# Two experts of one token in each gathered row block: expert sums with a 128-row contraction in a two-layer transformer kernel

## The chip, the cores and the metric

The kernel runs on one core of a Trainium2 chip, as one launch. The metric is the device time of that launch in microseconds, lower is better. All data are float32 (indices uint32).

## The reference

Two transformer layers run on 512 tokens of width 1024. Each layer has a mixer (layer 1: a state-space model and sliding-window attention; layer 2: a sparse attention and a short convolution) and then a retrieval of experts, which is what the change touches. For each token, 8 heads select 16 of 16,384 experts; with u and v the experts' rows of 1024 numbers:

```python
q = (xt @ w_query).reshape(t, PEER_HEADS, 2, PEER_KEY_DIM // 2)
s = einsum('thkd,hknd->thkn', q, sub_keys)
vals, idx = top_k(s, 16)                        # for each half of the key
best, pos = top_k(all 256 sums of the two halves' values, 16)
expert = i1 * 128 + i2 ; gate = softmax(best)   # 8 heads x 16 = 128 experts a token
a = einsum('cd,ced->ce', xb, u_tab[expert])     # one dot product per expert
w = gate * gelu(a)
out = einsum('ce,ced->cd', w, v_tab[expert])    # a weighted sum of the v rows
```

## The kernel before

The program is written by hand for each engine, and engines wait on semaphores. 512 tokens are 4 blocks of 128, two layers make 8 blocks n = 0..7, and each block has 128 **slots**, k = 0..127: 1024 slots in all, numbered s = 128 n + k.

One slot is one expert of each of the block's 128 tokens, with token p on partition p:

1. GpSimd (POOL) issues one indirect DMA that fetches 128 rows of 8 KB, u and v of an expert side by side, into a ring (L2263). It may do so when `idx` of the head is there, when `dot(s - 5)` is done (5 u places) and when `vmm(s - 10)` is done (10 v places).
2. VectorE (DVE) computes the dot product of the u row with the token's normalized input `xn` in one custom instruction (L409, function `dot`).
3. ScalarE (ACT) takes the gelu for a pair of slots and makes from it `diag`, a 128 x 64 tile: row p holds the weight in column p mod 64 and zeros elsewhere (`weigh`; all ACT activations stand under line L1198). `ident2` is the identity's two column halves added, and `gid` is `ident2` scaled by the gate.
4. TensorE (PE) multiplies `diag` by the v rows and adds into two PSUM banks (`vmm`, L1623). Tokens 0-63 and 64-127 are contracted apart, and the 1024 columns are taken in two halves, so a slot is four matmuls of 64 rows by 64 columns by 512, each on its own quarter of the array (`tile_position`). Every float32 matmul stands in the trace as two instructions and two weight loads: 8 and 8 a slot.

Beside the slots the same engines compute the mixers, the projections and the selection of the next blocks' experts. The order is fixed: `place` gives each part of that work a slot number, and `pace` and `slots` run the slots up to it first. TensorE runs four slots (`VL`) behind the dot products. SyncE streams weights of 512 KB into 6 places.

The parts that the change touches:

- `route(n)` (layer 1) and `route2(a)` (layer 2, two blocks at once) make X, the normalized input of block n, transpose it, project it and score it. X stands in `xn[:, n % 3, :]`.
- `top_part(n, h, q)` selects a head's 16 experts; its last instruction writes `idx` (L890). `gates(n, h)` writes `gate` (L466 in the profile, after a reciprocal in L856). On DVE `chained` and `wait_own` wait for the instruction before.
- the buffers `bmod`, `bmod2`, `cact` and `mrow` (a modulation vector, computed in block 0) lie in `xn`.

Of the kernel before, what the change touches and what calls it, by code (L numbers as in the profile page):

```python
# [104 lines left out]
def build(nc, A, out, act_counts):  # L105
    ctx = ExitStack()
    with ctx:
# [38 lines left out]
        xn = sb("xn", [128, 3, D])  # L146
# [63 lines left out]
        bmod2 = xn[:, 1, :].rearrange("p (a b) -> p a b", b=128)  # L210
        bmod, o = carve(xn[:, 2, :], 0, 4, 128)
        cact, o = carve(xn[:, 2, :], o, 8, 32)
        mrow = [carve(xn[:, 2, :], o + 128 * k, 128)[0] for k in range(2)]
# [185 lines left out]
        def vector_program(v):  # L399
            V = Lane("v", v, sems, book)  # L400

            def dot(s):
                n, k = divmod(s, 128)
                b = n % 2
                V.stage("dot")
                V.wait_ge("fetch", s)
                if k == 0 and n >= 2:
                    V.wait_ge("diag", 128 * (n - 1) - 1)
                V(v.tensor_tensor_reduce(u_row(s), u_row(s), xn[:, n % 3, :], 1.0, 0.0, ALU.mult, ALU.add,  # L409
                                         aw[:, b, k:k + 1]), ("dot", s))  # L410

# [27 lines left out]
            def slots(x):  # L439
                back = V.here  # L440
                while V.slot < x and V.slot < END:
                    c = V.slot
                    V.slot += 1
                    n, k = divmod(c, 128)
                    if c < NSLOT:
                        dot(c)
                    if c - 1 in turn_at:
                        finish(turn_at[c - 1])
                    if c in last_at:
                        finish2(last_at[c])  # L450
                    for m, h, q in tops.get(c, ()):
# [367 lines left out]
            def route(n):  # L819
                X = xn[:, n % 3, :]  # L820
                pace(n, "route", 0.0)
                V.stage("route")
                if n == 2:
                    V.wait_ge("modo", 10)
                    V.wait_ge("modo", 11)
# [10 lines left out]
                V(v.tensor_copy(xT[:, 4:8, :], P3(1)), ("XT", n, 1))  # L836
                pace(n, "route", 0.6)
# [12 lines left out]
            def gates(n, h):  # L850
                R = RB[n // 4]
                V.stage("top")
                V.wait_ge("g_exp", n, h)
                if h == 0 and n >= 2:
                    V.wait_ge("gid", 128 * (n - 1) - 1)
                V(v.reciprocal(R["zs"][:, h:h + 1], R["zs"][:, h:h + 1]))  # L856
                chained(lambda: ts(gate[:, n % 2, 16 * h:16 * h + 16], R["best"][:, h, :], R["zs"][:, h:h + 1], None,
                                   ALU.mult, None), ("gate", n, h))

            def top_part(n, h, q):  # L860
# [21 lines left out]
                if q == 3:  # L882
# [7 lines left out]
                    chained(lambda: v.scalar_tensor_tensor(idx[:, b, 16 * h:16 * h + 16], ee[:, 0, :], 128.0, ee[:, 1, :],  # L890
                                                           ALU.mult, ALU.add), ("idx", n, h))
# [233 lines left out]
            def route2(a):  # L1125
# [6 lines left out]
                for j in range(2):  # L1132
                    n = a + j
                    X = xn[:, n % 3, :]
# [8 lines left out]
                for j in range(2):  # L1143
                    n = a + j
                    pace(a, "route", 0.25 + 0.08 * j)
                    V.stage("route")
                    V.wait_ge("X_t", n, 1)
                    V(v.tensor_copy(XT[:, 4:8, 128 * j:128 * j + 128], P3((5, 3)[j])), ("XT", n, 1))
                for b in range(2):
# [43 lines left out]
        def scalar_program(a):  # L1193
# [32 lines left out]

            def evacuate(n):
# [26 lines left out]
            def slots(x):  # L1254
                back = S.here
                while S.slot < x and S.slot < END:
# [9 lines left out]
                    if c in last_at:  # L1266
                        finish2(last_at[c])
                    for m, h in exps.get(c, ()):
# [119 lines left out]
            def route(n):  # L1388
# [9 lines left out]
                S(act(xT[:, 0:4, :], P3(0), ACT.Copy), ("XT", n, 0))  # L1398
                if n == 0:
# [12 lines left out]
                pace(n, "route", 1.0)  # L1412

# [15 lines left out]
            def norm2(a):  # L1429
# [7 lines left out]
                S.stage("norm")  # L1437
                for j in range(2):
# [112 lines left out]
            def route2(a):  # L1551
# [7 lines left out]
                for j in range(2):  # L1559
# [4 lines left out]
                    S(act(XT[:, 0:4, 128 * j:128 * j + 128], P3((4, 2)[j]), ACT.Copy), ("XT", n, 0))  # L1564
                for b in range(2):
# [41 lines left out]
        def tensor_program(t):  # L1607
            T = Lane("t", t, sems, book)

            def vmm(s):  # L1610
# [294 lines left out]
            def route(n):  # L1905
                X = xn[:, n % 3, :]
# [252 lines left out]
            def route2(a):  # L2159
# [6 lines left out]
                for j in range(2):  # L2166
                    n = a + j
                    X = xn[:, n % 3, :]
# [314 lines left out]
```

## Time and profile before

| what | value |
|---|---|
| time, median of 3 runs | 3346.07 us (3346.05 to 3347.88) |
| the profiled execution | 3346.05 us, span of its instructions 3344.3 us |
| TensorE (PE) matmuls | 2489.2 us busy, 74% of the span |
| VectorE (DVE) | 2324.1 us, 69% |
| ScalarE (ACT) | 1328.9 us, 40% |
| GpSimd (POOL) | 1139.9 us, 34% |
| DMA | 1295.01 MB, mean 387 GB/s |
| mean granted TensorE clock | 0.836 |

A busy time is the time in which at least one instruction of the engine runs. Matmuls overlap, so their mean durations don't add up to it. The DMA share is the mean busy share of the core's 16 DMA engines; in dense stretches it reads slightly over 1. The granted clock is a share of 2.4 GHz: 0.5 is the level of 1.2 GHz and 1.0 that of 2.4 GHz.

### The profile page before, as it was taken

The numbers are of one execution on the slowest core, as the hardware profiler recorded it, in microseconds if no ns is written. First come the engines' busy times: TensorE is split into PE (matmuls) and PEld (weight loads), VectorE is DVE, ScalarE is ACT, GpSimd is POOL, SyncE is SP. The second block draws the span as 40 slices with busy tenths as digits, with TensorE's granted clock in tenths as the row PEclk, the third lists the DMA queues.
The fourth block names the chain that finished last, engine by engine and source line by source line (L and its number), as shares of the span: only waits on it lengthen the run. The fifth ranks groups of instructions, "written<-read, shape, count | busy, mean of one in ns | idle before, by whom it ended". The sixth has DMA issues, their size and how long they took to land.

```text
span 3344.3 us, 40597 instructions
## 1 busy us (share of the span) xinstructions
PE 2489.2 (74%) x14052; PEld 1065.7 (32%) x14052; DVE 2324.1 (69%) x5515; ACT 1328.9 (40%) x3602; POOL 1139.9 (34%) x1038
## 2 busy tenths in 40 slices
PE   8787778787797877969788759778887656555555
PEld 3443233223332233326343416423333211111111
DVE  6518785697947878385885585887866777777644
ACT  1213542444324444243473353357843343333322
POOL 0001343324323244242333343343433444444432
PEclk9698879898798987989788979877888877777776
DMA  7689999999999999999999999999999999999997
GB/s 228 204 305 393 417 394 406 405 409 414 383 394 418 414 404 382 404 399 385 371 381 393 382 408 365 413 411 416 369 409 363 406 420 419 418 410 414 419 420 323
DMA packets 214057, 1295.01 MB, mean 387 GB/s; under 512 B 26934, under 2 KB 30294, under 8 KB 82776
## 3 DMA queue, kind: packets, MB, share of 16 engines
q0 software_dynamic: 148320, 1076.50, 79.8%
q1 hardware_dynamic: 64860, 213.81, 16.9%
q8 instruction: 110, 1.80, 0.2%
q10 hardware_dynamic: 672, 2.12, 0.2%
q14 instruction: 95, 0.78, 0.1%
HBM read 1289.62 MB, written 2.71 MB: 386 GB/s over the span
## 4 chain that ended last, share of the span: by engine, by line
PE 34%; DMA 27%; DVE 21%; issue 9%; ACT 4%; POOL 3%; another core or an unknown queue 0%; POOLq 0%; ACTq 0%; DVEq 0%; SPq 0%
DMA ring<-in_k_uv,idx 11%; DMA ring<-in_k_vu,idx 11%; PE ps L1623 11%; PE ps L1703 10%; DVE ring L409 9%; DMA wsl<-in_k_wu 5%; PE ps L1959 5%; POOL ring L2263 3%; PE ps L1969 2%; DVE big L462 2%; ACT L1198 1%; PE ps L1680 1%; PE ps L1850 1%; DVE pers L462 1%; ACT diag L1198 1%
## 5 line engine op out<-in xcount | busy, mean ns | idle before, releaser
L1623 PE MATMUL ps<-ring,diag 64*64 64x512 f32 x8192 | 1264.4, 745 | 485.4 <-ACT diag L1198 460.0
L409 DVE CUSTOM_DVE_ANT_0 ring<-ring,xn 128x1024 f32<-128x1024 f32 x1024 | 1238.6, 1221 | 486.1 <-DMA ring<-in_k_vu,idx 260.2
L2263 POOL DMA_INDIRECT ring<-in_k_vu,idx x514 | 570.7, 1110 | 1144.0 <-DVE aw L409 635.5
L2263 POOL DMA_INDIRECT ring<-in_k_uv,idx x510 | 563.0, 1104 | 960.0 <-DVE aw L409 656.4
L1623 PEld LDWEIGHTS ps<-ring,diag 64*64 64x64 f32 x8192 | 315.6, 159 | 1266.6 <-ACT diag L1198 737.0
L1198 ACT ACTIVATE aw<-aw 128x2 f32<-128x2 f32 x512 | 103.7, 203 | 1086.2 <-DVE aw L409 1082.5
L1703 PE MATMUL ps<-wsl,xT 128*128 128x512 f32 x896 | 437.6, 633 | 31.5 <-DMA wsl<-in_k_wu 28.7
L1198 ACT ACT_TABLE_LOAD x338 | 433.7, 1283 | 11.9 <-DVE fin L436 5.2
L1198 ACT ACTIVATE diag<-gid,aw 128x64 f32<-128x64 f32 x1024 | 311.1, 342 | 302.1 <-PE ps L1623 285.1
L1198 ACT ACTIVATE gid<-ident,gate 128x64 f32<-128x64 f32 x1024 | 292.5, 333 | 0.0
L1703 PEld LDWEIGHTS ps<-wsl,xT 128*128 128x128 f32 x896 | 168.9, 199 | 296.6 <-issue 234.0
L1959 PE MATMUL ps<-pers,wsl 128*128 128x256 f32 x896 | 208.7, 393 | 25.1 <-DVE pers L467 17.8
L1959 PEld LDWEIGHTS ps<-pers,wsl 128*128 128x128 f32 x896 | 173.6, 196 | 72.0 <-issue 48.0
L1850 PE MATMUL ps<-pers,rowB 128*128 128x64 f32 x224 | 51.4, 422 | 72.3 <-DVE rowB L708 49.1
L409 DVE DVE_READ_ACCUMULATOR2_ANT aw<- 128x1 f32 x1024 | 84.6, 83 | 0.0
L1198 ACT ACTIVATE big<-ps 128x512 f32<-128x512 f32 (+4 forms) x58 | 30.2, 537 | 123.8 <-PE ps L1703 107.7
L1850 PEld LDWEIGHTS ps<-pers,rowB 128*128 128x128 f32 x224 | 48.8, 329 | 83.9 <-issue 83.9
L462 DVE TENSOR_TENSOR big<-ps,big 128x512 f32<-128x512 f32 x16 | 11.1, 692 | 78.4 <-PE ps L1703 78.4
L462 DVE TENSOR_TENSOR big<-big 128x512 f32<-128x512 f32 x68 | 47.1, 692 | 19.3 <-ACT big L1198 17.1
L1703 PE MATMUL ps<-wsl,fin 128*128 128x512 f32 x128 | 59.0, 604 | 0.9 <-DMA wsl<-in_k_wu 0.9
L2119 PE MATMUL ps<-pers 128*128 128x64 f32 x320 | 49.7, 307 | 12.4 <-DVE pers L1069 12.4
L2093 PE MATMUL ps<-pers,big 64*128 64x128 f32 (+3 forms) x128 | 54.8, 540 | 5.0 <-DVE big L462 5.0
(249 smaller groups left out, 2170.2 us busy)
## 6 DMA issues: line engine op xcount, KB each, us to landing
wsl<-in_k_wu SPq DMA_DIRECT2D x342, 512.0 KB
wsl<-in_k_wmod SPq DMA_DIRECT2D x48, 512.0 KB
ring<-in_k_vu,idx POOLq DMA_INDIRECT x514
ring<-in_k_uv,idx POOLq DMA_INDIRECT x510
wsl<-in_k_wu SPq DMA_DIRECT2D x8, 280.0 KB
hres<-in_x SPq DMA_DIRECT2D x4, 512.0 KB, 7.5
pers<-L1d POOLq DMA_DIRECT2D x8, 256.0 KB, 13.6
out<-fin ACTq DMA_DIRECT2D x4, 512.0 KB, 2.6
```

The costliest lines, as they stand in the source:

```text
L409: V(v.tensor_tensor_reduce(u_row(s), u_row(s), xn[:, n % 3, :], 1.0, 0.0, ALU.mult, ALU.add, aw[:, b, k:k + 1]), ("dot", s))
L462: return v.tensor_tensor(out, a_, b_, op)
L1198: return a.activation(out, in_, f, **kw)
L1623: r = t.matmul(PA[half][64 * q:64 * q + 64, :], diag[64 * half:64 * half + 64, s % (2 * PAIR), :], v_row(s)[64 * half:64 * half + 64, 512 ...
L1680: r = t.transpose(PS[bank][:, at + j * 128:at + (j + 1) * 128], s_, ident[:, :])
L1703: r = t.matmul(PS[bank][:, 0:nn], lhsT(kk_), wsl[:, at % NWS, j, 0:nn], start=(kk_ == 0 and not offset), stop=(kk_ == nk - 1))
L1850: x = t.matmul(PS[4 + h // 8][:, 64 * (h % 8):64 * (h % 8) + 64], PT1[:, r, 128 * k:128 * k + 128], v1[:, (n + 1 + k) % 2, 64 * g:64 * g + ...
L1959: r = t.matmul(PS[banks[c // 2]][:, 256 * (c % 2):256 * (c % 2) + 256], wsl[:, at % NWS, i, 128 * c:128 * c + 128], XT[:, kk_, :], start=( ...
L1969: r = t.matmul(PS[banks[j]][:, 0:nn], left(kk_)[:, 128 * j:128 * j + 128], wsl[:, at % NWS, i, 0:nn], start=(kk_ == 0), stop=(kk_ == nk - 1))
L2093: r = t.matmul(PS[k % 2][:, (h - h0) * Wk:(h - h0 + 1) * Wk], q2T[64 * g:64 * g + 64, h % 4, 128 * j:128 * j + 128], ksT[64 * g:64 * g + 6 ...
L2119: r = t.matmul(PS[4 + br][:, 64 * h:64 * h + 64], PT2[:, k % 2, at:at + 128], vsn[:, m, 128 * br + 64 * g:128 * br + 64 * g + 64], start=( ...
L2263: Q(p.indirect_dma_start(out=both_rows(s), out_offset=None, in_=tab, in_offset=bass.IndirectOffsetOnAxis(ap=idx[:, n % 2, k:k + 1], axis=0 ...
```

## The change

A slot now holds two experts of each of 64 tokens, no longer one expert of each of 128. In a head's 16 slots, the first 8 serve tokens 0-63: partitions 0-63 hold their experts c = 0..7, and partitions 64-127 the same tokens' experts 8..15. The other 8 slots serve tokens 64-127. `diag` already has two rows per column (p and p + 64), so one matmul over all 128 rows now adds both experts of a token. `vmm` issues two matmuls of 128 rows by 64 columns by 512 in place of four of 64 by 64 by 512.

For that, `idx` and `gate` have one quadrant moved between partition halves (three instructions in place of one for each, with waits). Each block's X needs two more versions, tokens 0-63 doubled and tokens 64-127 doubled: `doubled(n, half)` in `xd`, four rows of 1024 in place of three. For n = 0 to 4 and 6 they are made in the route part by `doubled_high` (ACT, one copy) and `doubled_low` (DVE, two copies). For n = 5 and 7 X waits in `xr`, and `doubled_late` makes them at the third slot of block n - 1 (ACT two copies, DVE two copies). Number and size of the gathers, dot products and diagonals stay.

```diff
-        xn = sb("xn", [128, 3, D])
+        xd = sb("xd", [128, 4, D])
...
+        def doubled(n, half):
+            return xd[:, 2 * (n % 2) + half, :]
...
-                if k == 0 and n >= 2:
-                    V.wait_ge("diag", 128 * (n - 1) - 1)
-                V(v.tensor_tensor_reduce(u_row(s), u_row(s), xn[:, n % 3, :], 1.0, 0.0, ALU.mult, ALU.add,
+                if k == 0:
+                    V.wait_ge("xb", n)
+                    if n >= 2:
+                        V.wait_ge("diag", 128 * (n - 1) - 1)
+                V(v.tensor_tensor_reduce(u_row(s), u_row(s), doubled(n, k // 8 % 2), 1.0, 0.0, ALU.mult, ALU.add,
                                          aw[:, b, k:k + 1]), ("dot", s))
+            def doubled_low(n):
+                X = doubled(n, 0)
+                V.wait_ge("X_t", n, 1)
+                V(v.tensor_copy(doubled(n, 1)[0:64, :], X[64:128, :]), ("xl", n))
+                V.wait_ge("xb0", n)
+                V.wait_own()
+                V(v.tensor_copy(X[64:128, :], X[0:64, :]))
+            def doubled_late(n):
+                V.stage("late")
+                V(v.tensor_copy(doubled(n, 0)[64:128, :], xr[0:64, :]))
+                V(v.tensor_copy(doubled(n, 1)[0:64, :], xr[64:128, :]), ("xl", n))
...
-                chained(lambda: ts(gate[:, n % 2, 16 * h:16 * h + 16], R["best"][:, h, :], R["zs"][:, h:h + 1], None,
-                                   ALU.mult, None), ("gate", n, h))
+                V.wait_own()
+                def out(p, to, c, src):
+                    g_ = gate[to:to + p, n % 2, 16 * h + c:16 * h + c + (16 if p == 128 else 8)]
+                    e_ = R["best"][src:src + p, h, 8 - c:16 - c] if p == 64 else R["best"][:, h, :]
+                    return ts(g_, e_, R["zs"][src:src + p, h:h + 1], None, ALU.mult, None)
+                V(out(128, 0, 0, 0))
+                V.wait_own()
+                V(out(64, 64, 0, 0))
+                V(out(64, 0, 8, 64), ("gate", n, h))
...   (idx in top_part: the same three instructions, in place of one)
+            def doubled_high(n):
+                S.wait_ge("X", n)
+                S(act(doubled(n, 1)[64:128, :], doubled(n, 0)[64:128, :], ACT.Copy), ("xb", n), ("xb0", n))
...   (ScalarE's doubled_late: waits for X and for dot 128 (n - 1) - 1, two such copies from xr)
-                for c in range(2):
-                    for half in range(2):
-                        q = (half + c) % 2
-                        r = t.matmul(PA[half][64 * q:64 * q + 64, :], diag[64 * half:64 * half + 64, s % (2 * PAIR), :],
-                                     v_row(s)[64 * half:64 * half + 64, 512 * q:512 * q + 512], start=(k == 0),
-                                     stop=(k == 127), tile_position=(64 * half, 64 * q))
+                half = k // 8 % 2
+                for q in range(2):
+                    r = t.matmul(PA[half][64 * q:64 * q + 64, :], diag[:, s % (2 * PAIR), :],
+                                 v_row(s)[:, 512 * q:512 * q + 512], start=(k in (0, 8)),
+                                 stop=(k in (119, 127)), tile_position=(0, 64 * q))
```

## Rows read from the trace of the kernel before

**Rows 1.** The page: busy engines, and DMA queues (packets, MB, share of 16 engines).

```profile
PE 2489.2 (74%) x14052; PEld 1065.7 (32%) x14052; DVE 2324.1 (69%) x5515; ACT 1328.9 (40%) x3602; POOL 1139.9 (34%) x1038
...
q0 software_dynamic: 148320, 1076.50, 79.8%
q1 hardware_dynamic: 64860, 213.81, 16.9%
```

**Rows 2.** Stretches: length, busy time (instructions) per engine, granted clock, DMA share, GB/s.

```profile
280.00:3322.00 3042.00, 2269.19 (x12671) 949.27 (x12669) 2187.49 (x5173) 1278.38 (x3494) 1128.96 (x1019) 0.84 0.99 401
3160.00:3320.00 160.00, 93.06 (x512) 21.04 (x508) 78.38 (x129) 40.55 (x160) 59.76 (x63) 0.73 1.01 420
```

**Rows 3.** Groups by form: busy us, mean ns of one, idle time before and its releasers.

```profile
L1623 PE MATMUL ps<-ring,diag 64*64 64x512 f32 x8192 | 1264.4, 745 | 485.4 <-ACT diag L1198 460.0 <-ACT xT L1198 16.8 <-ACT big L1198 6.8
L409 DVE CUSTOM_DVE_ANT_0 ring<-ring,xn 128x1024 f32<-128x1024 f32 x1024 | 1238.6, 1221 | 486.1 <-DMA ring<-in_k_vu,idx 260.2 <-DMA ring<-in_k_uv,idx 210.5 <-issue 14.3
```

**Rows 4.** Timeline of TensorE in five places: start us, length us, how many instructions.

```profile
3304.24 3.69 PE L1623 MATMUL ps<-ring,diag 64*64 64x512 f32 x16 [1.30 <-ACT diag L1198]
3309.21 1.95 PE L1623 MATMUL ps<-ring,diag 64*64 64x512 f32 x16 [1.28 <-ACT diag L1198]
...
549.50 1.09 PE L1623 MATMUL ps<-ring,diag 64*64 64x512 f32 x8
550.52 3.70 PE L1703 MATMUL ps<-wsl,xT 128*128 128x512 f32 x8
...
167.80 1.52 PE L1870 MATMUL ps<-wsl,xn 128*32 128x128 f32 x48
```

**Rows 5.** Groups by form again: small VectorE writes, copies on VectorE and ScalarE.

```profile
L890 DVE SCALAR_TENSOR_TENSOR idx<-rowB 128x16 uint32<-128x16 f32 x32 | 5.6, 175 | 1.1
...
L466 DVE TENSOR_SCALAR gate<-rowB 128x16 f32<-128x16 f32 x32 | 7.5, 234 | 1.3 <-DVE rowB L856 0.2
...
L623 DVE COPY big<-big 128x512 f32<-128x512 f32 x4 | 1.7, 427 | 0.1
...
L1198 ACT ACTIVATE xr<-hres 128x1024 f32<-128x1024 f32 x14 | 14.7, 1048 | 56.6 <-DVE hres L462 42.7 <-DVE xn L462 11.5 <-DMA hres<-in_x 2.4
```

**Rows 6.** Timeline of VectorE around the first indices and gates.

```profile
256.06 0.69 DVE L889 TENSOR_REDUCE rowB<-rowB 128x32 f32<-128x512 f32 x1
256.78 0.17 DVE L890 SCALAR_TENSOR_TENSOR idx<-rowB 128x16 uint32<-128x16 f32 x1
256.88 0.48 DVE L462 TENSOR_TENSOR xn<-ps,xn 128x128 f32<-128x128 f32 x2
...
266.63 0.23 DVE L466 TENSOR_SCALAR gate<-rowB 128x16 f32<-128x16 f32 x1
266.78 0.29 DVE L462 TENSOR_TENSOR xn<-ps,xn 128x128 f32<-128x128 f32 x1
274.70 0.29 DVE L462 TENSOR_TENSOR xn<-ps,xn 128x128 f32<-128x128 f32 x1 [7.64 <-PE ps L1870]
```

**Rows 7.** Stretches, columns as in rows 2: two selections, three where the DMA share falls.

```profile
283.00:359.00 76.00, 73.03 (x245) 25.66 (x244) 72.17 (x246) 34.38 (x76) 17.25 (x18) 0.95 0.98 397
686.00:755.00 69.00, 57.52 (x203) 19.00 (x202) 63.30 (x211) 31.13 (x70) 14.88 (x16) 0.90 1.02 408
...
1480.00:1500.00 20.00, 12.48 (x57) 8.78 (x58) 18.61 (x52) 7.44 (x21) 6.18 (x5) 0.74 0.92 370
...
2000.00:2020.00 20.00, 14.67 (x64) 10.58 (x65) 15.65 (x46) 4.51 (x14) 6.36 (x6) 0.74 0.77 286
2540.00:2560.00 20.00, 15.02 (x92) 5.40 (x88) 17.20 (x41) 8.09 (x21) 7.86 (x6) 0.73 0.66 234
```

**Rows 8.** Timeline of all engines in the route part of blocks 6 and 7.

```profile
2535.33 3.78 PE L1711 MATMUL ps<-big,ones 1*128 1x512 f32 x4 [12.22 <-DVE big L1130]
...
2541.81 1.22 DVE L409 CUSTOM_DVE_ANT_0 ring<-ring,xn 128x1024 f32<-128x1024 f32 x1
...
2543.31 0.94 POOL L2263 DMA_INDIRECT ring<-in_k_vu,idx  x1 [10.45 <-DVE aw L409]
```

More of the change, by code:

```diff
@@ L209, in build @@
         av = xr
[L210 to L213, printed above, removed]
+        bmod2 = xd[:, 2, :].rearrange("p (a b) -> p a b", b=128)
+        bmod, o = carve(xd[:, 3, :], 0, 4, 128)
+        cact, o = carve(xd[:, 3, :], o, 8, 32)
+        mrow = [carve(xd[:, 3, :], o + 128 * k, 128)[0] for k in range(2)]
         hn = cols2[:, 0:20]
@@ L450, in slots @@
                         finish2(last_at[c])
+                    if k == 2 and n in L2_PARTS:
+                        doubled_late(n + 1)
                     for m, h, q in tops.get(c, ()):
@@ L819, in route @@
             def route(n):
-                X = xn[:, n % 3, :]
+                X = doubled(n, 0)
                 pace(n, "route", 0.0)
                 V.stage("route")
-                if n == 2:
-                    V.wait_ge("modo", 10)
-                    V.wait_ge("modo", 11)
                 rstd(n, "r", 1, D)
@@ L836, in route @@
                 V(v.tensor_copy(xT[:, 4:8, :], P3(1)), ("XT", n, 1))
+                if n == 1:
+                    V.wait_ge("modo", 10)
+                    V.wait_ge("modo", 11)
+                doubled_low(n)
                 pace(n, "route", 0.6)
@@ L889, in top_part, with out @@
                     chained(lambda: v.tensor_reduce(ee, oh, AXX, ALU.add))
-                    chained(lambda: v.scalar_tensor_tensor(idx[:, b, 16 * h:16 * h + 16], ee[:, 0, :], 128.0, ee[:, 1, :],
-                                                           ALU.mult, ALU.add), ("idx", n, h))
+                    V.wait_own()
+                    def out(p, to, c, src):
+                        i_ = idx[to:to + p, b, 16 * h + c:16 * h + c + (16 if p == 128 else 8)]
+                        e_ = ee[src:src + p, :, 8 - c:16 - c] if p == 64 else ee
+                        return v.scalar_tensor_tensor(i_, e_[:, 0, :], 128.0, e_[:, 1, :], ALU.mult, ALU.add)
+                    V(out(128, 0, 0, 0))
+                    V.wait_own()
+                    V(out(64, 64, 0, 0))
+                    V(out(64, 0, 8, 64), ("idx", n, h))
             def top(n, h, at):
@@ L1148, in route2 @@
                     V(v.tensor_copy(XT[:, 4:8, 128 * j:128 * j + 128], P3((5, 3)[j])), ("XT", n, 1))
+                pace(a, "route", 0.45)
+                V.stage("route")
+                doubled_low(a)
                 for b in range(2):
@@ L1225, in weigh, with doubled_late @@
                         gated(PAIR * g + PAIR + j)
+            def doubled_late(n):
+                S.stage("late")
+                S.wait_ge("X", n)
+                S.wait_ge("dot", 128 * (n - 1) - 1)
+                S(act(doubled(n, 0)[0:64, :], xr[0:64, :], ACT.Copy))
+                S(act(doubled(n, 1)[64:128, :], xr[64:128, :], ACT.Copy), ("xb", n))
             def evacuate(n):
@@ L1267, in slots @@
                         finish2(last_at[c])
+                    if k == 2 and n in L2_PARTS:
+                        doubled_late(n + 1)
                     for m, h in exps.get(c, ()):
@@ L1398, in route @@
                 S(act(xT[:, 0:4, :], P3(0), ACT.Copy), ("XT", n, 0))
+                if n == 1:
+                    S.wait_ge("modo", 10)
+                    S.wait_ge("modo", 11)
+                doubled_high(n)
                 if n == 0:
@@ L1437, in norm2 @@
                 S.stage("norm")
+                if a == 6:
+                    S.wait_ge("xl", a - 1)
                 for j in range(2):
@@ L1905, in route @@
             def route(n):
-                X = xn[:, n % 3, :]
+                X = doubled(n, 0)
                 pace(n, "route", 0.0)
```

7 lines of the change are left out of this document (5 added, 2 removed).

## The prediction

> **What bounds the kernel now.** I read the page first, for who is busy, then the stretches, for what is full when, and then the timeline, because a busy share doesn't say who waits for whom. The page shows no engine full: TensorE 74%, VectorE 69%. The two DMA queues together show 79.8 + 16.9 = 96.7% of all 16 engines' span [rows 1]. The stretches say the same by time. From 280 us, when the gathers are running, to the last gather at 3322 us, the DMA share is 0.99; from 3160 to 3320 us, where slots alone run, it is 1.01 at 420 GB/s, which is what "full" reads like here [rows 2]. Its 512 matmul instructions, at 8 a slot, are 64 slots in 160 us: 2.5 us a slot, while VectorE is busy 78 us of the 160 and TensorE 93 us [rows 2]. Of the 486 us in which VectorE stands idle before dot products, 471 end with the landing of a gather [rows 3]. So a slot costs the time to fetch 1 MB, and the kernel is bound by its 1295 MB. What can be won between 280 and 3322 us without moving fewer bytes is what is missing from full: (1.01 - 0.99) x 3042 = 61 us by rounded shares. From the stretches where the share falls I read off (1.01 - 0.92) x 20 = 1.8, (1.01 - 0.77) x 20 = 4.8 and (1.01 - 0.66) x 20 = 7.0 us [rows 7]; the holes are short and scattered over the routes and projections. An edit to the slots can thus win little, and it loses only if it delays gathers so far that the queue runs dry.
>
> **TensorE: matmuls halved, time kept.** The edit removes half of the L1623 matmuls (8 to 4 instructions a slot, 8192 to 4096) [rows 3]. What matters is how the old ones run. At the full clock, one slot's 8 instructions take 1.09 us, two slots' 16 take 1.95 us, so a further slot adds 0.86 us; 8 instructions over the whole array (128 by 128) take 3.70 us one after the other, a pitch of about 0.43 us [rows 4]. 0.86 is two such pitches: the four quarter-array matmuls already run side by side, in two rounds (a float32 matmul is two instructions). The new slot has two half-array matmuls, each again two instructions of 512 columns, hence again two rounds if the halves run side by side. Do they? No 128 by 64 pair is in the trace. The nearest row is L1870, 128 rows by 32 columns on four column positions: 48 instructions of 128 columns take 1.52 us [rows 4]. A pitch for 128 columns is 0.43/4 = 0.11 us; 48 in a row would need 5.2 us; 12 rounds of four need 1.3 us and the tail of the last one, which is the 1.52. So column positions with all 128 rows do run side by side, four of them. Bounds: below, two rounds less what half the issue could save, at the least one round, 0.43 us, a slot; above, no overlap, 4 x 0.43 = 1.72 us. I take 0.86, no change, as L1870 is very near. At the 1.2 GHz level two slots take 3.69 us [rows 4], and I expect the same there.
>
> The Trainium skill, "TensorEngine Tiling (Array Packing)", section Performance Considerations, "Instruction Overhead", says that each matmul carries some 60 cycles of overhead. By it, four instructions fewer a slot would save 240 cycles, an estimate of 0.10 us at 2.4 GHz, 102 us of TensorE time over 1024 slots. The rows speak against adding that up: 0.86 us for two rounds leaves no room for it. If the rule held, the faster rival below would be the outcome.
>
> **VectorE: index and gate.** For each of 64 heads (8 blocks x 8), `idx` gets two more writes and one wait, `gate` the same. One `idx` write is 0.175 us, one `gate` write 0.234 us [rows 5]. They overlap what follows if it doesn't depend on them: the instruction after `idx` starts 0.10 us after it, the one after `gate` 0.15 us; a dependent one starts 0.03 us after the end (256.06 + 0.69 to 256.78) [rows 6]. So `idx` goes from 0.10 to 0.175 + 0.035 + 0.10 + 0.10 = 0.41 us, +0.31; `gate` from 0.15 to 0.234 + 0.035 + 0.15 + 0.15 = 0.57, +0.42. Without any overlap they would be +0.385 and +0.50. I take 0.75 us a head (0.73 to 0.89), 48 us in all.
>
> **Copies.** Six routes with two VectorE copies and one ScalarE copy, two late ones with two and two: 16 VectorE and 10 ScalarE copies of 64 x 1024. Nearest: 128 x 512 within SBUF at 0.427 us, so 0.8 us for twice the columns; ScalarE 128 x 1024 at 1.05 us [rows 5]. That makes 13 us on VectorE and 10.5 us on ScalarE. `doubled_low` also waits for ScalarE's copy (`xb0`); ScalarE issues it right after its own transposed copy, so 0 to 1 us. Behind the waiting VectorE stand the next dot products, and behind these the gathers five slots on.
>
> **What of these 61 us of VectorE work shows.** A gather has to be issued before the queue is empty, so a delay counts only where VectorE has no idle time to absorb it and the queue has no gather waiting.
>
> - The start. The first gather waits for the first head's `idx`: +0.3 us. Gates and second head add 1.2 us more, but VectorE then idles 7.64 us for TensorE [rows 6]. 0.3 us (0 to 1.5).
> - The selection of six heads during the input projection of blocks 1 to 3. Here VectorE is the tightest: 72.2 of 76 us busy, 63.3 of 69 [rows 7], and the rest is gaps between chained instructions. Six heads add 4.5 us each time. Yet the DMA share is 0.98 to 1.02 meanwhile [rows 7], since weights fill in, and TensorE (73.0 of 76) is nearly full too. Were nothing hidden it would cost 3 x 4.5 = 13.5 us, and all hidden 0. The full DMA decides: I take 1 us each, 3 us.
> - The six routes. 1.6 us of copies and up to 1 us of wait. In the last one the queue does run dry: VectorE waits for TensorE's L1711, the dot product follows at 2541.81, the gather is issued after 10.45 us [rows 8], and the share is 0.66 [rows 7]. The copies come after this hole, when gathers are being caught up. 0 to 2.6 us each, at most 16; I take 2 us for all six.
> - The other selections run beside slots that leave VectorE idle about half the time [rows 2]. The late copies come 126 slots before their use, and so does each wait for `xb` at a block's first dot product, whose X is made in the route before. The wait for `modo`, moved from the route of block 2 to that of block 1 (about 590 us), is for small writes of block 0, whose last matmuls (L1870) ended before 274.7 us [rows 6]. All of these 0.
>
> Were the cover gone everywhere, all 61 us would show. ScalarE at 40% [rows 1] has room for its 10.5 us.
>
> Sum: the profiled execution took 3346.05 us, 3344.3 of span and 1.75 around it; the median of the runs is 3346.07, the same. 3346.05 + 0 + 0.3 + 3 + 2 = 3351.35. I say **3351 us**, 0.15% above. A change within 0.2% (6.7 us: 3339.4 to 3352.8) is about what a measurement of this kernel cannot tell from none.
>
> **The rivals.**
>
> - *TensorE unchanged, VectorE's additions mostly hidden* (forecast): 3343 to 3353, as the holes of the queue may shift by a few us either way.
> - *VectorE's additions uncovered* (slower). For it: 95% busy in the selection and queues that do run dry in routes. Against: full DMA in the same stretches. It gives up to 1.5 + 13.5 + 16 = 31 us, 3377; half of it 3362. It decides from 7 us of uncovered work, a ninth of the 61.
> - *TensorE gets shorter per slot* (faster): if the half-array matmuls needed fewer than two rounds, up to 0.43 us a slot. For it: gathers also wait for vmm(s - 10), and in the hole at 2000 us TensorE is busy 14.7 of 20 us with VectorE at 15.7 [rows 7], so that either may be what is late. It would fill the holes of 1480 and 2000 us, 1.8 + 4.8 us, and their like; at most all 61. I put it at 12 to 20 us less, less the 5 above: about 3335. Against: the 0.86 us and L1870 [rows 4].
> - *The two halves run one after the other* (much slower): 1.72 us a slot, 0.86 x 1024 = 881 us more of TensorE, 2489 + 881 = 3370 us, over the whole span, before any wait: at least 3420 us. Against it: L1870.
> - *It doesn't do what it says*: the matmul count halves by construction, so only the time can fail to follow; that is the forecast.
>
> **Chances.** Forecast 0.52, VectorE uncovered 0.31, one after the other 0.04, TensorE shorter 0.13 (of it 0.10 beyond 0.2%, 0.03 within). Slower by over 0.2%: 0.31 + 0.04, and 0.02 of the forecast's edge: 0.37. Faster 0.10. Same 0.53. The range takes the lower bound of the faster case's likely part and of the slower one to a good half: 3335 to 3366. For the likeliest case alone it is 3343 to 3355.
>
> **What would show it.** TensorE: L1623 with 4096 matmuls of form 128 by 64, two slots in 1.9 to 2.0 us at the full clock and its busy time near 1264 us. If it is near 650, the faster rival holds; near 2100, the serial one. VectorE: busy time up by about 60 us, L890 with 64 x 3 instructions. DMA: share 0.99 from 280 to 3322 us, 2.5 us a slot at the end. If the share in 283 to 363 us falls below 0.96, VectorE is uncovered there; if it does so after 590, 980, 1380, 1840 and 2555 us, it is the copies. The prediction is wrong above all if something I costed at zero moves the clock or the DMA rate, as every number hangs on 420 GB/s.

## The result, and the profile after

The changed kernel takes 3363.66 us (median of 7 runs, 3355.54 to 3369.52), the kernel before on the same chip 3342.52 us (3331.29 to 3347.88). The ratio, which is estimated over more executions than these seven and so is not quite the quotient of the two medians, is 1.0057, 95% interval 1.0040 to 1.0074: 19 us slower (13 to 25). That is inside the range of 3335 to 3366 us, but in the case "slower by over 0.2%", to which the prediction gave 0.37, and not in the forecast's "same".

One execution of each kernel was profiled, and such single ones differ by up to 14 us either way (the change 3346 to 3370 us in 22 of them, the kernel before 3326 to 3354 in the experiments). The profiled execution of the change took 3354.14 us with a span of 3352.7, 8.4 us over the span before. The page, as in [rows 1]:

```profile
PE 2460.7 (73%) x9956; PEld 1039.1 (31%) x9956; DVE 2395.3 (71%) x5787; ACT 1338.6 (40%) x3612; POOL 1142.0 (34%) x1038
...
q0 software_dynamic: 148320, 1076.50, 79.6%
q1 hardware_dynamic: 64860, 213.81, 16.8%
```

The bytes are the same to the last digit. TensorE has 4096 matmuls fewer and VectorE 71.2 us more to do (2395.3 - 2324.1). The groups by form, which answer to [rows 3]:

```profile
L1689 PE MATMUL ps<-ring,diag 128*64 128x512 f32 x4096 | 1248.6, 743 | 521.4 <-ACT diag L1242 483.4
L416 DVE CUSTOM_DVE_ANT_0 ring<-ring,xd 128x1024 f32<-128x1024 f32 x1024 | 1236.7, 1221 | 427.7 <-DMA ring<-in_k_vu,idx 230.7 <-DMA ring<-in_k_uv,idx 188.9 <-issue 4.4
```

Half the matmuls keep TensorE busy for 1248.6 us in place of 1264.4. About half of these 16 us goes with the clock and not with the form: this execution was granted 0.841, the one before 0.836, and executions with the old form at 0.841 took 1254.8 (e9) and 1258.4 us (e6). The dot product takes 1221 ns as before. VectorE now stands idle 419.6 us (230.7 + 188.9) for gathers where it was 470.7: of its 71 us of new work, 51 went into idle time that it had at dot products. TensorE's timeline, which answers to [rows 4], has the same stages at both clock levels:

```profile
548.39 1.08 PE L1689 MATMUL ps<-ring,diag 128*64 128x512 f32 x4
...
3309.26 1.94 PE L1689 MATMUL ps<-ring,diag 128*64 128x512 f32 x8 [1.52 <-ACT diag L1242]
3314.25 3.61 PE L1689 MATMUL ps<-ring,diag 128*64 128x512 f32 x8 [3.04 <-ACT diag L1242]
```

A slot takes 1.08 us and two take 1.94, so the second adds 0.86 us, as before; at the 1.2 GHz level two take 3.61 us, before 3.69.

Where is the time, then? The stretches (columns as in rows 2), first the long one and the one at the end, then two of the three in which six heads are selected beside an input projection, then two in which the queue runs low:

```profile
280.00:3333.00 3053.00, 2242.33 (x8585) 922.87 (x8583) 2253.71 (x5428) 1287.09 (x3503) 1131.11 (x1019) 0.84 0.99 399
3170.00:3330.00 160.00, 90.89 (x256) 19.75 (x254) 78.34 (x129) 40.55 (x160) 59.60 (x63) 0.75 1.01 420
...
279.00:359.00 80.00, 73.18 (x182) 25.61 (x180) 75.27 (x263) 32.07 (x72) 16.68 (x18) 0.95 0.97 386
685.00:757.00 72.00, 61.45 (x158) 19.85 (x156) 67.75 (x232) 31.32 (x70) 14.34 (x16) 0.91 1.02 405
...
1600.00:1620.00 20.00, 14.26 (x60) 8.10 (x60) 12.02 (x38) 4.52 (x16) 5.02 (x5) 0.86 0.75 294
2545.00:2565.00 20.00, 13.94 (x46) 5.38 (x48) 13.74 (x28) 10.90 (x24) 4.06 (x4) 0.76 0.70 266
```

At the end, where slots alone run, nothing has changed: 256 matmuls at 4 a slot are 64 slots in 160 us, 2.5 us a slot, at 420 GB/s. The first selection takes 80 us in place of 76 and has 0.97 and 386 GB/s where it had 0.98 and 397 [rows 7]. Its six heads begin their `idx` writes at 294.1 to 358.6 us before and at 290.7 to 361.0 us after, one per 12.9 and one per 14.1 us: here the 1.15 us that a head has more (see e12) shows in full in the pace of the selection, though e5 will tell that less of it reaches the end. The rounded share of 0.99 over the long stretch is no longer fine enough. GB/s is finer, because both kernels move the same bytes. Five stretches of the kernel before:

```profile
280.00:800.00 520.00, 424.30 (x2025) 164.38 (x2023) 396.82 (x991) 215.84 (x555) 169.83 (x153) 0.88 1.00 405
800.00:1400.00 600.00, 472.71 (x2458) 197.73 (x2462) 436.18 (x949) 230.57 (x640) 206.21 (x184) 0.87 1.00 400
1400.00:2000.00 600.00, 460.46 (x2860) 233.53 (x2852) 415.97 (x1014) 276.68 (x742) 221.82 (x194) 0.87 0.99 389
2000.00:2560.00 560.00, 455.61 (x2736) 223.74 (x2740) 421.29 (x1016) 298.88 (x720) 216.69 (x192) 0.83 0.97 392
2560.00:3160.00 600.00, 361.04 (x2080) 108.36 (x2076) 437.83 (x1077) 215.85 (x680) 254.66 (x234) 0.77 1.01 414
```

and the same five of the change:

```profile
280.00:800.00 520.00, 422.38 (x1411) 161.29 (x1409) 408.35 (x1041) 217.21 (x558) 170.24 (x154) 0.88 1.00 402
800.00:1400.00 600.00, 465.68 (x1714) 191.26 (x1714) 440.52 (x972) 226.34 (x628) 204.12 (x182) 0.86 0.99 397
1400.00:2000.00 600.00, 461.56 (x2073) 230.93 (x2074) 425.43 (x1044) 276.66 (x734) 217.52 (x191) 0.86 0.97 385
2000.00:2560.00 560.00, 445.27 (x1966) 213.97 (x1962) 432.61 (x1071) 302.91 (x730) 218.09 (x193) 0.85 0.98 395
2560.00:3160.00 600.00, 350.29 (x1152) 104.38 (x1152) 461.86 (x1163) 220.89 (x687) 257.81 (x233) 0.79 1.00 412
```

What a stretch lost is the difference of the rates over the rate after, times its length: 3/402 x 520 = 3.9 us, then 3/397 x 600 = 4.5, 4/385 x 600 = 6.2, -3/395 x 560 = -4.3 and 2/412 x 600 = 2.9, together 13 us. Four of five stretches share the loss, each with more VectorE work in it (11.5, 4.3, 9.5 and 24.0 us), and the granted clock is the same within 0.02. Two executions alone could differ so by chance, so here are the same stretches in the profiles of the experiments. Four kernels that lose nothing that can be seen (before, e2, e3, e7) have 400 to 404 GB/s in the second stretch, 389 to 391 in the third and 412 to 415 in the last; the change again (e4) and three kernels with small writes alone (e1, e11, e12) have 397 to 399, 383 to 388 and 410 to 412. The first and the fourth don't tell the two sets apart. So the loss is in no one place: the three that show it reach from 800 to 3160 us. What is lost stays lost to the end, since the slots there have no slack. (13 us is more than the 8.4 of the spans. The first gather happened to start at 254.26 us in this execution and at 257.87 before, and what follows the last slot was a little shorter.)

The waits of GpSimd (us in total, times, longest) say who holds the gathers back. Before:

```profile
POOL ring L2263 <- DVE aw L409: 1291.9, 533, 20.8
POOL ring L2263 <- PE ps L1623: 451.5, 188, 10.1
```

and after:

```profile
POOL ring L2329 <- DVE aw L416: 1347.4, 539, 21.0
POOL ring L2329 <- PE ps L1689: 396.9, 175, 9.9
```

Gathers wait 55 us longer for dot products and 55 us less for TensorE, and most of those waits are harmless, with transfers still queued. This difference says little: the profile of e2, which costs nothing that can be seen, has 1332.2 and 413.8 us, and that of e12, which costs 18 us, 1313.8 and 435.5. To which engine the lateness moved can't be read from these sums.

### The profile page after: what moved, and what is told of

Its sections match the earlier page's. It is cut to its first block, busy times and chain, and to the rows that moved or that the text cites. A ratio compares the mean times of both kernels' runs of the same rounds, so it can differ in the third digit from the quotient of the medians.

```text
span 3352.7 us, 32695 instructions
## 1 busy us (share of the span) xinstructions
PE 2460.7 (73%) x9956; PEld 1039.1 (31%) x9956; DVE 2395.3 (71%) x5787; ACT 1338.6 (40%) x3612; POOL 1142.0 (34%) x1038
## 4 chain that ended last, share of the span: by engine, by line
PE 33%; DVE 26%; DMA 22%; issue 9%; ACT 4%; POOL 3%; SPq 0%; another core or an unknown queue 0%; POOLq 0%; ACTq 0%; DVEq 0%
DMA ring<-in_k_uv,idx 11%; PE ps L1689 10%; DVE ring L416 10%; PE ps L1769 9%; DMA ring<-in_k_vu,idx 9%; PE ps L2025 5%; POOL ring L2329 3%; DMA wsl<-in_k_wu 3%; PE ps L2035 2%; DVE big L486 2%; ACT L1242 1%; PE ps L1916 1%; PE ps L1746 1%; DVE rowB L486 1%; DVE pers L486 1%
## 5 line engine op out<-in xcount | busy, mean ns | idle before, releaser
L1689 PE MATMUL ps<-ring,diag 128*64 128x512 f32 x4096 | 1248.6, 743 | 521.4 <-ACT diag L1242 483.4
L416 DVE CUSTOM_DVE_ANT_0 ring<-ring,xd 128x1024 f32<-128x1024 f32 x1024 | 1236.7, 1221 | 427.7 <-DMA ring<-in_k_vu,idx 230.7
L1689 PEld LDWEIGHTS ps<-ring,diag 128*64 128x64 f32 x4096 | 297.6, 162 | 1301.5 <-ACT diag L1242 752.5
L1746 PE MATMUL ps<-ident,xr 128*128 128x128 f32 x160 | 33.9, 376 | 45.4 <-DVE xr L490 22.7
## 6 DMA issues: line engine op xcount, KB each, us to landing
pers<-L1d POOLq DMA_DIRECT2D x8, 256.0 KB, 12.4
```

The costliest lines, as they stand in the source:

```text
L416: V(v.tensor_tensor_reduce(u_row(s), u_row(s), doubled(n, k // 8 % 2), 1.0, 0.0, ALU.mult, ALU.add, aw[:, b, k:k + 1]), ("dot", s))
L1689: r = t.matmul(PA[half][64 * q:64 * q + 64, :], diag[:, s % (2 * PAIR), :], v_row(s)[:, 512 * q:512 * q + 512], start=(k in (0, 8)), stop= ...
L1746: r = t.transpose(PS[bank][:, at + j * 128:at + (j + 1) * 128], s_, ident[:, :])
```

## The experiments

All were timed against the kernel before on the same chip; a difference in us is the ratio less 1 times the median of before there (3341.09 in e1 to e4, 3342.02 in e5 to e8, 3339.28 in e9 to e11, 3340.92 in e12).

### e1 to e4: which part of the change costs

Three suspects: (A) the small writes of `idx` and `gate`, (B) the copies of X, (C) the new form of the matmul. Each was put alone into the kernel before, with the change itself beside them.

**e1, small writes alone.** Each head's `idx` and `gate` get a wait and two more half writes, each half from itself, so that nothing moves (the edit is shown without the switches by which later runs vary it):

```diff
-                                                           ALU.mult, ALU.add), ("idx", n, h))
+                                                           ALU.mult, ALU.add))
+                    V.wait_own()
+                    for p, c in ((64, 0), (0, 8)):
+                        V(v.scalar_tensor_tensor(idx[p:p + 64, b, 16 * h + c:16 * h + c + 8],
+                                                 ee[p:p + 64, 0, c:c + 8], 128.0, ee[p:p + 64, 1, c:c + 8],
+                                                 ALU.mult, ALU.add), *([("idx", n, h)] if c == 8 else []))
...   (gate: the same)
```

> The kernel before, with the four small VectorE writes a head (two of idx, two of gate, with the waits) added, each rewriting the values that stand there. Theory A (the small writes in the selections are what isn't covered): slower by most of the whole change's 19 us, 12 to 19 us, ratio 1.0036 to 1.0057. Theory B (the copies in the routes): within 3 us. Theory C (the matmuls' new form): within 3 us. VectorE busy up by about 50 us in all cases.

Measured: 3353.99 us, ratio 1.0041 (1.0026 to 1.0057), 13.7 us slower. The groups of e1 by form show what was added:

```profile
L466 DVE TENSOR_SCALAR gate<-pers 64x8 f32<-64x8 f32 x64 | 18.5, 289 | 2.2
L466 DVE TENSOR_SCALAR gate<-rowB 64x8 f32<-64x8 f32 x64 | 15.1, 236 | 2.2
L903 DVE SCALAR_TENSOR_TENSOR idx<-pers 64x8 uint32<-64x8 f32 x64 | 10.3, 161 | 2.1
L903 DVE SCALAR_TENSOR_TENSOR idx<-rowB 64x8 uint32<-64x8 f32 x64 | 10.3, 161 | 2.1
```

These 256 instructions of 512 elements add up to 54.2 us, and VectorE's busy time rose by 51.8 us (2324.1 to 2375.9). By these medians they cost three quarters of what the whole change does.

**e2, copies alone.** The copies at their places and with their waits; they write into a spare buffer `xs`, and the dot products still read `xn`:

```diff
+            def doubled_low(n):
+                X = xn[:, n % 3, :]
+                V.wait_ge("X_t", n, 1)
+                V(v.tensor_copy(xs[0:64, :], X[64:128, :]))
+                V.wait_ge("xb0", n)
+                V.wait_own()
+                V(v.tensor_copy(xs[0:64, :], X[0:64, :]))
...   (doubled_late, ScalarE's copies and the wait for xb at k == 0 as in the change)
```

> The kernel before, with the copies of X alone (16 on VectorE, 10 on ScalarE, and their waits), into a tile that nothing reads. Theory A: within 4 us of the kernel before. Theory B: slower by 12 to 19 us. Theory C: within 3 us.

Measured: 3343.62 us, ratio 1.0008 (0.9994 to 1.0023), +2.7 us with zero inside the interval. The six early pairs take 732 and 687 ns a copy, the two late ones 689 and 682:

```profile
L418 DVE COPY xs<-xn 64x1024 f32<-64x1024 f32 x6 | 4.4, 732 | 0.2
L421 DVE COPY xs<-xn 64x1024 f32<-64x1024 f32 x6 | 4.1, 687 | 0.6
```

The idle time before the second group, which holds the wait for `xb0`, is 0.6 us for all six: that wait costs nothing. Three things of the change are not in e2: the copies there all write partitions 0 to 63 on VectorE, so half of them move nothing; the waits for `modo` stay where they were; and X of blocks 5 and 7 doesn't go through `xr`.

**e3, matmul form alone.** `vmm` as in the change over the old data; since a slot still holds 128 tokens, each output adds up rows of two tokens, so this is a measure of time alone:

```diff
-                for c in range(2):
-                    for half in range(2):
-                        q = (half + c) % 2
-                        r = t.matmul(PA[half][64 * q:64 * q + 64, :], diag[64 * half:64 * half + 64, ...
+                half = k // 8 % 2
+                for q in range(2):
+                    r = t.matmul(PA[half][64 * q:64 * q + 64, :], diag[:, s % (2 * PAIR), :], ...
```

> The kernel before with the new vmm alone: two matmuls of 128 rows by 64 columns in place of four of 64 by 64. The weighted sum of the experts is not the reference's (the rows of two tokens are added). Theories A and B: two slots in 1.95 us of TensorE at the full clock as before, time within 3 us. Theory C: slower by over 10 us. If TensorE gained from fewer instructions, faster by 3 us or more.

Measured: 3338.63 us, ratio 0.9988 (0.9976 to 1.0000), 4 us less (0 to 8). Its matmuls stand at

```profile
L1622 PE MATMUL ps<-ring,diag 128*64 128x512 f32 x4096 | 1245.3, 741 | 492.5 <-ACT diag L1198 473.9 <-ACT xT L1198 13.6 <-ACT big L1198 5.1
```

which is 19 us under the 1264.4 of [rows 3], but that execution had a granted clock of 0.836 and this one 0.843. With the old form, e2 took 1250.4 us at 0.844 and e10 1253.0 at 0.843, so the form itself is worth 5 to 8 us of TensorE time.

**e4, the change again**, without an edit.

> The whole change once more, on the same chip as the parts: by the comparison so far 13 to 25 us slower. If the parts add up, it is the sum of the three other runs within 4 us.

Measured: 3358.31 us, ratio 1.0056 (1.0037 to 1.0076), +18.7 us. So (A) holds as the largest part, (B) is small, and (C) costs nothing and may give a little back, its interval ending at zero.

### e5 and e6: where do small writes cost

The prediction let added VectorE work show only where VectorE is nearly full. The small writes were put into the 18 heads that are selected during the input projections (e5), and into the other 46 (e6). The edit is that of e1 under a condition:

```diff
+                    if (n < 3 and h >= 2):          # e6: if not (...)
```

> The small VectorE writes of the earlier run, for 18 of the 64 heads alone: heads 2 to 7 of blocks 0, 1 and 2, which are selected during the input projections of blocks 1 to 3. VectorE busy up by some 14 us. Theory A1 (only where VectorE has no idle time does a write show): slower by most of the 13.7 us (ratio 1.0041) of all 64 heads, at least 8 us. Theory A2 (every added write shows in part, wherever it is): 18/64 of it, 4 us.

> The same writes for the other 46 heads alone, some 36 us more of VectorE. Theory A1: within 4 us of the kernel before. Theory A2: slower by 46/64 of 13.7 us, 10 us.

Measured: e5 3347.13 us, ratio 1.0016 (1.0002 to 1.0029), 5.3 us. e6 3351.72 us, ratio 1.0025 (1.0007 to 1.0043), 8.4 us. The two make 13.7, as e1 does; with 4 to 6 us either way on each that is luck. "Only in the tight selections" asked for at least 8 us in e5 and at most 4 in e6. Both medians speak against it, and both intervals (0.7 to 9.7 and 2.3 to 14.4 us) still reach into it. What e6 does show is that the 46 heads beside which VectorE has idle time cost more than nothing. Per head the measures are 0.30 and 0.18 us, and their intervals (0.04 to 0.54, 0.05 to 0.31) do not tell them apart.

### e7 and e8: the gate's writes on ScalarE

If small writes on VectorE cost, it should help to put them on ScalarE, which is at 40%. In e7 the one `gate` write of the kernel before is moved there, in e8 the change's three; here that of e8 (each then stands a few slots later in ScalarE's order):

```diff
-                V(out(128, 0, 0, 0))
-                V.wait_own()
-                V(out(64, 64, 0, 0))
-                V(out(64, 0, 8, 64), ("gate", n, h))
+            def gate_out(n, h):
+                S.wait_ge("g_rc", n, h)
...   (out: the same, as an activation with a scale)
+                S(out(128, 0, 0, 0))
+                S.wait_own()
+                S(out(64, 64, 0, 0))
+                S(out(64, 0, 8, 64), ("gate", n, h))
```

> The kernel before, with the gate's write moved from VectorE to ScalarE (VectorE keeps the reciprocal, ScalarE writes gate from best and zs, two slots later). VectorE is relieved of 0.15 us a head at its margin, ScalarE gets some 0.2 us. Theory A1: VectorE's time in the selections shows one to one, so 18 x 0.15 = 2.7 us faster. Rival (VectorE's order, not its load, sets the gathers): no change, or slower where ScalarE is late.

> The whole change, with the gate's three writes on ScalarE and not on VectorE. VectorE's small writes fall from four a head to the two of idx. Theory A1: of the whole change's 18.7 us (1.0056) the gate's part of the small writes, over half of 13.7 us, goes away: 8 to 11 us slower than the kernel before. Rival (ScalarE is then late with the gates): 15 us or more slower.

Measured: e7 3341.52 us, ratio 1.0002 (0.9986 to 1.0017): no difference that can be seen. VectorE was busy 15.3 us less (2308.8), of which a quarter would be 4 us, inside the interval. e8 3349.58 us, ratio 1.0022 (1.0010 to 1.0035), 7.4 us slower than before in place of e4's 18.7: with VectorE at 2344.2 us, 51 under the change, about 11 us came back. This is the remedy of largest effect here, and still no version that beats the kernel before.

### e9 to e11: how the cost grows

After e5 and e6 the nearest theory was A2: about a quarter of any VectorE work added here shows. Rivals: any edit shifts the queue's holes once (A3), slack is used up and the rest shows in full (A4), blocks 0 to 3 alone pay (A5). e9 makes each small write of e1 twice (`for again in range(2):`), e10 has them for `n >= 4` alone, e11 is e1 again beside them.

> The kernel before, with the small writes of e1 made twice: for all 64 heads, idx and gate each get four more instructions (64 x 8) and two more waits, where e1 added two and one. Results unchanged. VectorE gets about 2 x 52 = 104 us of busy time more than before. Theory A2 (a constant share of added VectorE time shows, 13.7 of 52 us in e1): 2 x 13.7 = about 27 us, ratio 1.008 (1.006 to 1.010). Rival A3 (the cost is not of VectorE's time but a shift in the pattern of the queue's holes, which any edit brings once): about the same 14 us as e1, ratio 1.003 to 1.005. Rival A4 (slack is used up, so that the second portion shows in full): 14 + 52 = 66 us, ratio about 1.02.

> The kernel before, with e1's small writes only for the 32 heads of blocks 4 to 7 (layer 2), none of which is selected during an input projection. Results unchanged. VectorE +26 us. Theory A2: half of e1, 7 us, ratio 1.002 (1.001 to 1.0035). Rival A5 (blocks 0 to 3 alone pay, where VectorE is 88 to 95% busy): 0 to 2 us, ratio 1.000 to 1.0006.

> e1 once more, beside e9 and e10 on the same chip: two more small writes for idx and two for gate in all 64 heads of the kernel before. Under any theory about the 14 us of e1, ratio 1.003 to 1.005; it is here to be the single portion beside e9's double one.

Measured: e9 3375.06 us, ratio 1.0105 (1.0082 to 1.0127), 35.1 us; e10 3345.64 us, 1.0019 (1.0001 to 1.0037), 6.3 us; e11 3356.02 us, 1.0048 (1.0029 to 1.0066), 16.0 us. Double work cost 2.2 times as much, which leaves A3 and A4 out; half the heads, all in layer 2, cost 0.4 times as much, which speaks against A5 but does not rule it out, as the interval of e10 holds A5's 1.0006. VectorE's busy time rose by 99.5 us in e9:

```profile
PE 2462.6 (73%) x14052; PEld 1057.1 (31%) x14052; DVE 2423.6 (72%) x6027; ACT 1328.3 (39%) x3602; POOL 1148.5 (34%) x1038
```

so 35% of it showed (28 to 43), where e1 had 26% and e11 31%. A2 is the nearest of them, though 1.0105 lies just above its 1.006 to 1.010, and only the interval reaches into it; whether the share grows with the amount these intervals don't tell.

### e12: the move between halves

One thing was left: parts of 13.7 + 2.7 - 4.0 = 12.4 us against a whole of 19, though with some 5 us either way on each this could be noise. The trace of VectorE around a late head shows a difference between the small writes of e1 and of the change. In each fence the first row is the `idx` write and the next line the instruction behind it, in the kernel before:

```profile
2926.96 0.17 DVE L890 SCALAR_TENSOR_TENSOR idx<-pers 128x16 uint32<-128x16 f32 x1
2927.05 1.22 DVE L409 CUSTOM_DVE_ANT_0 ring<-ring,xn 128x1024 f32<-128x1024 f32 x1
```

in e1:

```profile
2893.92 0.17 DVE L897 SCALAR_TENSOR_TENSOR idx<-pers 128x16 uint32<-128x16 f32 x1
2894.13 0.35 DVE L903 SCALAR_TENSOR_TENSOR idx<-pers 64x8 uint32<-64x8 f32 x2
2894.41 1.21 DVE L409 CUSTOM_DVE_ANT_0 ring<-ring,xn 128x1024 f32<-128x1024 f32 x1
```

and in the change:

```profile
2900.68 0.57 DVE L928 SCALAR_TENSOR_TENSOR idx<-pers 128x16 uint32<-128x16 f32 x3
2901.28 1.23 DVE L416 CUSTOM_DVE_ANT_0 ring<-ring,xd 128x1024 f32<-128x1024 f32 x1
```

From the first write to the dot product it is 0.09, 0.49 and 0.60 us. Before, the dot product starts 0.08 us before the write's end, in e1 0.07 before the end of the last; in the change it starts 0.03 us after it. e12 puts the change's exact writes, quadrants moved, into the kernel before (`out` of the change's diff, nothing else):

> The kernel before with exactly the change's three writes of idx and of gate in all 64 heads, that is with the quadrants moved between partition halves (source in one half, destination in the other), where e1 wrote each half from itself. Nothing else is changed; since the slots still read idx and gate in the old order, the experts are fetched for other tokens, so this is a measure of time alone. In the trace of the change a dot product after the idx writes starts 0.60 us after the first of them (2900.68 to 2901.28), in e1 0.49 us (2893.92 to 2894.41), in the kernel before 0.09 us (2926.96 to 2927.05). Theory M: it is the move between halves that keeps the next instruction from overlapping the last write, so 0.60 us is seen here too, and a head costs about 1.15 us more than before in place of e1's 0.93; by e1's and e11's 14 to 16 us that makes 17 to 20 us, ratio 1.005 to 1.006, which is all that the whole change costs but the copies. Rival N: what follows in the change's program (its buffers, its input order) keeps it; then 0.49 us is seen here and the ratio is e1's, 1.004 to 1.005.

Measured: 3356.58 us, ratio 1.0054 (1.0034 to 1.0074), 18.0 us. Its trace:

```profile
2900.99 0.56 DVE L903 SCALAR_TENSOR_TENSOR idx<-pers 128x16 uint32<-128x16 f32 x3
2901.58 1.23 DVE L409 CUSTOM_DVE_ANT_0 ring<-ring,xn 128x1024 f32<-128x1024 f32 x1
```

0.59 us: M's reading, not N's 0.49, and so it is with 62 of the 64 heads of e12, where the next instruction starts 0.03 us or more after the end of the last `idx` write. The ratio lies in the range of M too, but by itself would not tell it from e1's. The parts now come nearer: 18.0 (e12) + 2.7 (e2) - 4.0 (e3) = 16.7 us, beside 18.7 (e4) and 19.1 of the whole, each of them with some 5 us either way.

The move is not the whole rule, though. Of the two half writes of e1, which move nothing, the second starts 0.03 us after the end of the first in every head (two of 0.16 us take the 0.35 above), so these don't overlap either. And the two heads of e12 that are left are followed by a copy out of PSUM, which starts 0.08 us before the end of a moved write, as with 2181.97 + 0.16 and 2182.05 us. What these cases have in common, no run here varies by itself.

## Why the prediction was right or wrong, step by step

- **What bounds the kernel**: held. Bytes and the 2.5 us a slot at the end are unchanged, and what was lost is lost as rate between 280 and 3160 us. But the conclusion drawn from it, that an edit "loses only if it delays gathers so far that the queue runs dry", was read as if that were rare. It happens in small measure in many places.
- **TensorE 0**: right in size and reason, a slot's pitch of 0.86 us in both forms. e3 measured -4 us (-8 to 0), with 5 to 8 us less of matmul busy time at the same clock. By the Trainium skill, "TensorEngine Tiling (Array Packing)", Performance Considerations, "Instruction Overhead", each matmul has an overhead of some 60 cycles; added to every matmul, that would have shown as an estimated 0.10 us a slot at 2.4 GHz. The trace shows 0.86 us with 8 instructions and with 4, so it does not agree with that reading for matmuls that run side by side. The same section of the Trainium skill says that a matmul over one column takes as long as one over 60; if the overhead is meant as such a least time, no run here, with 512 columns in each, bears on it.
- **Small writes 0.75 us a head, 48 us**: too small. In busy time it was 0.81 us a head in e1 (51.8/64) and 0.94 with the change's own writes in e12 (60.2/64, from 2384.3 us). In time by which the next instruction is later it was more: `idx` 0.60 - 0.09 = 0.51 us where I had 0.31, and `gate` 0.64 where I had 0.42, by the first head of the change:

```profile
263.63 0.76 DVE L490 TENSOR_SCALAR gate<-rowB 128x16 f32<-128x16 f32 x3
264.42 0.29 DVE L486 TENSOR_TENSOR xd<-ps,xd 128x128 f32<-128x128 f32 x1
```

  0.79 us to the next start, less the 0.15 of [rows 6]. So 1.15 us for this head, 74 us if all were like it. I had let each new write overlap its follower as the old one did. But the second half write starts 0.03 us after the end of the first, even in e1 where nothing moves, and in the change the next instruction waits for the end of the last as well. Of the 0.20 us that `idx` took beyond my term, each of the two makes about half (e1 has 0.40, e12 0.50).
- **Copies 13 us on VectorE, 2 us visible**: right. 4.4 + 4.1 + 1.4 + 1.4 = 11.3 us of work, +2.7 us (-2 to 8) seen, an interval that would have held 0 or 7 us as well.
- **What shows of it: 0.3 + 3 + 2, all else 0**: this is the step that failed. "The other selections run beside slots that leave VectorE idle about half the time ... All of these 0" met 8.4 us (2.3 to 14.4) in e6 for 46 heads, and "I take 1 us each, 3 us" for the tight selections met 5.3 us (0.7 to 9.7) in e5, which does not contradict it. The small writes as the change has them cost 18.0 us where 3.3 were taken for them. The mean idle time of VectorE (half, from a stretch in which slots alone run) says nothing on whether it is late at the moment. There are long parts of other work between dot products, longer than the 2.5 us of a slot. Before the `idx` write of the late head shown in e12 it is 2.8 us, from

```profile
2924.17 0.08 DVE L409 DVE_READ_ACCUMULATOR2_ANT aw<- 128x1 f32 x1
2924.29 0.25 DVE L466 TENSOR_SCALAR pers<-pers 128x16 uint32<-128x16 uint32 x2
```

  to the dot product at 2927.05. The work added stands in just these parts. Of VectorE's added busy time 26% (e1), 31% (e11), 30% (e12) and 35% (e9) reached the end, as an average over all places. That it does so by way of late gathers and a queue that runs dry fits the GB/s by stretch; no single late gather was followed to the end.
- **The rivals**: the forecast (0.52, 3343 to 3353 us) fell, and "VectorE's additions uncovered" (0.31, from 7 us up, half of it 3362) came true, by its size. That the measured 3363.66 lies in the range of 3335 to 3366 us is owed to the half of this rival that the range takes in, and in part to luck: its places were the wrong ones, routes (2.7 us with all copies, e2) and tight selections (5.3 us, e5) where by e6 the other heads cost most. "TensorE shorter", "one after the other" and "doesn't do what it says" fell. (The 3420 us of "one after the other" is 50 us over the 3370 that its own sum gives, and nothing is named for them.)
- **What would show it**: TensorE's four signs came as written. VectorE +60 came as +71. The first selection's share fell to 0.97, above the 0.96 that I had set as the sign of uncovered work, and the long stretch still read 0.99: both signs were too coarse for 0.5%. GB/s over equal bytes was fine enough.

What stays open: which of the queue's holes grew, whether layer 2 pays as much per head as layer 1, and what part of the cost goes with the clock. The slower kernels also had a lower granted clock, by the medians of their executions 0.836 for the change, 0.836 in e1, 0.837 in e12 and 0.838 in e9 and e11, where the kernel before had 0.839 to 0.841. Among executions of one and the same kernel the slower ones have the lower clock too; by an estimate from that scatter (9 us for each 0.01), 0.002 to 0.005 would be 2 to 5 us of the 14 to 35. Whether the clock is there the cause or the consequence, no run shows. Single executions scatter by more than a hole, so the few us of e5, e6 and e10 were told from medians and not located in a trace. It was also not tried to make `idx` without the move.

## What to carry to other kernels

In a kernel that is bound by a queue with holes, do not price added work by the mean idle time of its engine: take a share of all of it, in this kernel a quarter to a third, and let the zero be only the lower bound. (How large the share is in another kernel no run here says.) Count 512-element instructions with the fixed time that they take (0.16 to 0.29 us each on average here), since moving a few elements on an engine that is often late can cost more than halving the matmuls of another gives. To see half a per cent in a profile of equal bytes, compare GB/s by stretch, not rounded shares, and do it over several profiles. To see what a new form of matmul does to TensorE's time, compare executions with the same granted clock: here 0.836 against 0.843 alone made over 10 us of busy time.

## What the runs showed of the hardware that was not expected

- After a VectorE write that takes its source from one partition half and puts it into the other, the next instruction started 0.03 us after its end, and 0.07 us before its end where each half was written from itself (e12 against e1, 62 of 64 `idx` writes). Exceptions go both ways: a half write that moves nothing started 0.03 us after the end of one on the other half (e1, all 64 heads), and a copy out of PSUM started 0.08 us before the end of a moved write (e12, two heads). Why is not shown.
- Half the partitions and half the columns are not cheaper: `gate` 64 x 8 took 236 and 289 ns on average (e1; single ones 222 to 424), where 128 x 16 took 234 [rows 5]; `idx` 64 x 8 took 161 where 128 x 16 took 175.
- Two half-array matmuls (128 rows by 64 columns) take the same time as four quarter-array ones (64 by 64) over the same columns: 1.94 and 1.95 us for two slots at 2.4 GHz, 3.61 and 3.69 at 1.2 GHz. Over the whole kernel the two took 5 to 10 us less of 1250 at the same granted clock (e3 against e2 and e10, the change against e6 and e9).
